# Head biases of an attention built once in an earlier layer and loaded by transfers

## The reference

```python
DILATED_GROUPS = ((128, 1), (512, 4), (2048, 16))
delta = u + BLOCK - kk
band = (delta >= 0) & (delta <= window // dilation)
bias = -slopes[:, None, None] * (delta * dilation).astype(jnp.float32)[None]
sc = jnp.where(valid[:, None, None], sc + bias, -jnp.inf)
...
x = x + _rms_norm(mix, g[1])
ff = _swiglu(_rms_norm(x, g[2]), ffn_in_w[layer], ffn_out_w[layer])
x = x + _rms_norm(ff, g[3])
```

## Time and profile before

| | us |
|---|---|
| median of the runs | 2267.86 (2267.3 to 2268.08) |
| the profiled execution | 2266.35 |
| its span | 2264.6 |
| PE busy | 98% of the span |
| DVE busy | 74% |
| ACT busy | 43% |
| POOL busy | 21% |
| mean granted clock of PE | 0.997 |

### The profile page before, as it was taken

The page is one execution under the profiler, slowest core; times in us unless marked ns, Lnnn a source line. Parts: engine busy times, 40 slices in busy tenths (PEclk is TensorE's granted clock), DMA queues, the critical chain, the costliest instruction groups (busy, mean ns, idle before and its releaser), DMA issues. The chain is left out here.

```text
span 2264.6 us, 31165 instructions
## 1 busy us (share of the span) xinstructions
PE 2218.9 (98%) x10682; PEld 1855.2 (82%) x10682; DVE 1686.4 (74%) x2529; ACT 962.9 (43%) x1758; POOL 485.5 (21%) x416
## 2 busy tenths in 40 slices
PE   9999998999999999999999999999899999999998
PEld 7888887888888888877888888888788888888886
DVE  6988759777777667797677666676877777776768
ACT  4322345232222343564666566565533333323453
POOL 5000026333333100251000001002633333310113
PEclk9999999999999999999999999999999999999999
DMA  5122341333333487635333333234133333338774
GB/s 159 38 56 56 114 142 57 109 108 97 109 96 111 158 265 242 205 121 164 85 85 85 68 73 84 57 108 144 53 111 112 98 107 103 103 110 280 247 228 172
DMA packets 246013, 278.37 MB, mean 123 GB/s; under 512 B 18528, under 2 KB 157792, under 8 KB 243808
## 3 DMA queue, kind: packets, MB, share of 16 engines
q1 hardware_dynamic: 242656, 264.84, 38.4%
q10 hardware_dynamic: 3200, 11.54, 1.5%
HBM read 202.40 MB, written 48.76 MB: 111 GB/s over the span
## 5 line engine op out<-in xcount | busy, mean ns | idle before, releaser
L1256 PE MATMUL banks<-xb_mid,up_split 128*128 128x512 f32 x2064 | 477.5, 391 | 1.5 <-DVE up_split L2388 1.5
L1256 PEld LDWEIGHTS banks<-xb_mid,up_split 128*128 128x128 f32 x2064 | 388.5, 188 | 82.3 <-DVE up_split L2388 1.7
L1345 PE MATMUL banks<-down_split 128*128 128x512 f32 x1848 | 422.9, 390 | 4.6 <-DVE down_split L2756 3.2
L1345 PEld LDWEIGHTS banks<-down_split 128*128 128x128 f32 x1848 | 345.5, 188 | 80.6 <-DVE down_split L2756 7.7
L1256 PE MATMUL banks<-xb_low,up_split 128*128 128x512 f32 x1584 | 367.5, 390 | 5.7 <-DVE xb_low L2316 2.0
L1256 PEld LDWEIGHTS banks<-xb_low,up_split 128*128 128x128 f32 x1584 | 297.0, 188 | 68.8 <-DVE up_split L2388 5.4
L2756 DVE TENSOR_TENSOR down_split<-down_raw,down_split 128x1024 fp32r<-128x1024 f32 x154 | 198.1, 1287 | 107.7 <-ACT down_split L1963 107.4
L1963 ACT CAST down_split<-down_raw 128x1024 fp32r<-128x1024 f32 x154 | 162.1, 1053 | 204.0 <-PE banks L1345 168.6
L3397 POOL TENSOR_TENSOR sums<-raw_up 128x512 f32<-128x512 f32 x88 | 117.0, 1332 | 481.5 <-DMA raw_up<-in_ffn_in_w 255.4
L1390 PE MATMUL banks<-x_hi,w_second 128*128 128x512 f32 x672 | 176.4, 394 | 0.0
L3069 DVE CUSTOM_DVE_ANT_0 scores<-banks,bias 128x896 f32<-128x896 f32 (+7 forms) x128 | 96.7, 756 | 73.3 <-PE banks L1427 64.1
(11 more groups left out here) (229 smaller groups left out, 3616.7 us busy)
## 6 DMA issues: line engine op xcount, KB each, us to landing
raw_up<-in_ffn_in_w SPq DMA_DIRECT2D x88, 512.0 KB, 5.0
down_raw<-in_ffn_out_w SPq DMA_DIRECT2D x154, 256.0 KB, 3.4
down_raw<-hid_spill SPq DMA_DIRECT2D x154, 256.0 KB, 4.1
hid_spill<-hid_mix SPq DMA_DIRECT2D x110, 256.0 KB, 4.7
down_second<-in_ffn_out_w SPq DMA_DIRECT2D x66, 256.0 KB, 3.4
k_stack<-k_parts SPq DMA_DIRECT2D x32, 512.0 KB, 6.3
hid_spill<-hid SPq DMA_DIRECT2D x44, 256.0 KB, 2.0
raw_up<-in_conv_in_w SPq DMA_DIRECT2D x18, 512.0 KB, 5.1
```

Source lines behind the costliest of these rows:

```text
L1256: mm = pe.matmul(bank(b_out), up_part(ph, p, a)[:, q * P:(q + 1) * P], block(RIGHT_OF[p], b)[:, q, :], start=(i == 0), stop=(i == len(pass ...
L1345: mm = pe.matmul(bank(b_out), side[:, a, 0, i * P:(i + 1) * P], side[:, b, 1, :], start=(p in (M3, M5, M1, M2) and first and j == 0), stop ...
```

## The change

The tables move from the opening of attention into up0. There the residual stream `resid` lies idle, so its eight tiles are stored to `x_keep`, and the tables take its place. POOL makes the iota in set 2; DVE works through 22 parts in sets 3 to 13, three in an odd set (two in set 13) and one in an even one: six parts for `dist`, the counts and the logarithms, then one part for each of the 16 heads, a full bias of 128x1024 in one instruction into one of two slots of `head_table`, which SP stores to `bias_spill`. In sets 15 to 18 SP loads the tiles of `resid` back. In attention `bias` has two slots, one for each head of a pair, filled by SP (`load_bias`): the first two behind the last transpose of norm2, the others behind the last maximum of the head that used the slot. DVE only waits for them; `head_bias`, `last_bias` and `slope` go. Before the last pair the second chunk of output weights is loaded ahead of the pair's first bias. The order `OPENING` is as before.

```diff
+        dist_i = at(112, "dist_i", [SEQ], I32)
+        neg_log = at(116, "neg_log", [SEQ])
+        counted = at(124, "counted", [2, SEQ])
+        head_table = at(136, "head_table", [2, SEQ])
+        TABLE_SETS, TABLE_PARTS, TILES_BACK = range(3, 14), 6, {15: (0, 1), 16: (2, 3), 17: (4, 5), 18: (6, 7)}
+        def table_parts(n):
+            before = 4 * ((n - 3) // 2) + (3 if n % 2 == 0 else 0)
+            return before, {2: 0, 3: 1, 4: 2} if n % 2 and n < 13 else {2: 0, 3: 1} if n % 2 else {3: 0}
...
+                if layer == 0:
+                    for t in range(TT):
+                        sp.wait_ge(*x_new_right.at("norm1", t + 1))
+                        sp.dma_start(x_keep[t], resid[:, t, :]).then_inc(kept, 16)
...
+                            if j >= TABLE_PARTS:
+                                head = j - TABLE_PARTS
+                                sp.wait_ge(*bias_made.at("up0", head + 1))
+                                sp.dma_start(bias_spill[head], head_table[:, head % 2, :]) \
+                                    .then_inc(bias_out[head % 2], 16)
+                    if layer == 0 and n in TILES_BACK:
...
+                        for t in TILES_BACK[n]:
+                            sp.dma_start(resid[:, t, :], x_keep[t]).then_inc(x_back, 16)
...
+            def load_bias(r, e):
+                moving, fixed = r
+                if fixed:
+                    sp.wait_ge(*max_done.at("attn", moving * STEPS + (fixed * STEPS - (1 - e) * TT)))
...
+                sp.dma_start(att["bias"][:, e, :], rows[bass.ds(moving * (2 * P) + (2 * fixed + e) * P, P), :]) \
+                    .then_inc(bias_in[e], 16)
...
-            for pos in range(2, 5):
+            for pos in range(2, 4):
                 load_projection(pos)
+            sp.wait_ge(*xt_turned.at("norm2", TT))
+            for e in range(2):
+                load_bias((0, 0), e)
+            load_projection(4)
             stack_first()
             for pair in range(PAIRS - 2):
                 load_projection(6 + 3 * pair)
                 load_projection(7 + 3 * pair)
                 stack_keys((0, pair + 1), 0)
+                load_bias((0, pair + 1), 0)
                 load_projection(8 + 3 * pair)
                 stack_queries((0, pair + 1), 0)
                 stack_keys((0, pair + 1), 1)
+                load_bias((0, pair + 1), 1)
                 stack_queries((0, pair + 1), 1)
             load_row_block("oproj", o_w[0], 0)
             stack_keys((0, PAIRS - 1), 0)
             load_row_block("oproj", o_w[0], 1)
+            load_bias((0, PAIRS - 1), 0)
             stack_queries((0, PAIRS - 1), 0)
             stack_keys((0, PAIRS - 1), 1)
+            load_bias((0, PAIRS - 1), 1)
...
+                    head = j - TABLE_PARTS
+                    if head >= 2:
+                        dve.wait_ge(bias_out[head % 2], 16 * (head // 2))
+                    dve.scalar_tensor_tensor(out=head_table[:, head % 2, :], in0=dist,
+                                             scalar=2.0 ** (-(head % 2 + 1) / 2 - head // 2), in1=logs,
+                                             op0=ALU.mult, op1=ALU.add).then_inc(bias_made.sem, 1)
...
-                    in1=att["bias"][:, SEQ - n:SEQ], scale=1.0, scalar=3e38,
+                    in1=att["bias"][:, place(s, last)[1], SEQ - n:SEQ], scale=1.0, scalar=3e38,
...
-                        head_bias(moving, fixed + (s + 1) // STEPS, (s + 1) // TT % 2, 0)
+                    if s + 1 in (TT, STEPS):
+                        dve.wait_ge(bias_in[(s + 1) // TT % 2],
+                                    moving * 16 + 16 * (fixed + (s + 1) // STEPS + 1))
...
-            distances()
-            window_counts(0)
-            window_counts(1)
             project((0, 0), 2, OPENING)
             prepare(chunk0["attn"] + 3)
             values_low((0, 0), 0, TURN)
-            window_counts(2)
             project((0, 0), 3, OPENING)
-            masked_logs()
-            log_of(2)
             prepare(chunk0["attn"] + 4)
             values_low((0, 0), 1, TURN)
-            log_of(3)
-            head_bias(0, 0, 0, 0)
-            head_bias(0, 0, 0, 1)
             project((0, 0), 5, OPENING)
+            dve.wait_ge(bias_in[0], 16)
             negated_scores(0, 0)
...
+                    if ph == "up0" and n == 2:
+                        pool.wait_ge(kept, 16 * TT)
...
+                        pool.iota(dist_i[:], pattern=[[-1, SEQ]], base=SEQ - P, channel_multiplier=1) \
+                            .then_inc(dist_ready.sem, 1)
```

More of the change, by code:

```diff
@@ L331, in trunk @@
         spilled, stored = sem("spilled"), sem("stored")
+        kept, x_back = sem("kept"), sem("x_back")
+        bias_out = [sem(f"bias_out{i}") for i in range(2)]
+        bias_in = [sem(f"bias_in{e}") for e in range(2)]
         k_stacked = [sem(f"k_stacked{e}") for e in range(2)]
@@ L843, in load_ffn @@
                         store_mixed(up, n - 1)
+                    if layer == 0 and n in TABLE_SETS:
+                        before, places = table_parts(n)
+                        for j in range(before, before + len(places)):
+                            if j >= TABLE_PARTS:
[4 more added lines that the diff above has]
+                    if layer == 0 and n in TILES_BACK:
+                        for b in range(2):
+                            sp.wait_ge(bias_out[b], 16 * PAIRS)
+                        sp.wait_ge(kept, 16 * TT)
+                        for t in TILES_BACK[n]:
+                            sp.dma_start(resid[:, t, :], x_keep[t]).then_inc(x_back, 16)
                     store_hidden(up, n)
@@ L2792, in mix, with table, window_counts @@
                 ins.then_inc(mix_made.sem, 1)
+            dist, logs, bits = dist_f[:], neg_log[:], window_bits[:]
+            rest, count = counted[:, 0, :], counted[:, 1, :]
+            tables = [0]
+            def table(ins):
+                ins.then_inc(table_step.sem, 1)
+                tables[0] += 1
+                dve.wait_ge(*table_step.at("up0", tables[0]))
+            def window_counts(n):
+                window, dilation = DILATED_GROUPS[n]
+                this = rest if n else count
+                if dilation == 1:
+                    table(dve.tensor_scalar(this, dist, float(window), None, ALU.is_le))
+                else:
+                    table(dve.tensor_scalar(bits, dist_i[:], dilation - 1, None, ALU.bitwise_and))
+                    table(dve.tensor_scalar(this, bits, 0.0, None, ALU.is_equal))
+                    if window < SEQ:
+                        table(dve.scalar_tensor_tensor(out=this, in0=dist, scalar=float(window),
+                                                       in1=this, op0=ALU.is_le, op1=ALU.mult))
+                if n:
+                    table(dve.tensor_tensor(count, count, rest, ALU.add))
@@ new lines, in distances, with masked_logs, log_of @@
+            def distances():
+                dve.wait_ge(*dist_ready.at("up0", 1))
+                table(dve.tensor_copy(dist, dist_i[:]))
+            def masked_logs():
+                table(dve.scalar_tensor_tensor(out=count, in0=dist, scalar=0.0, in1=count,
+                                               op0=ALU.is_ge, op1=ALU.mult))
+                table(dve.tensor_scalar(logs, count, 0.0, MASKED, ALU.is_equal, ALU.mult))
+            def log_of(c):
+                table(dve.tensor_scalar(rest, count, float(c), -float(np.log(c)),
+                                        ALU.is_equal, ALU.mult))
+                table(dve.tensor_tensor(logs, logs, rest, ALU.add))
@@ L2828, in up_layer @@
                         split_low(down, 1)
+                    if layer == 0 and n in TABLE_SETS:
+                        before, places = table_parts(n)
+                        if p in places:
+                            table_part(before + places[p])
                     if n and n % 2 and p == 1:
@@ L3115, in attend @@
                     project((0, fixed), 5)
-                    biases = 0
                     for s in range(STEPS):
-                        if s + 1 in (HT, TT, TT + HT):
-                            dve.wait_ge(*max_done.at("attn", steps + (s + 1)))
-                            for part in range(1 if s + 1 == HT else 2):
-                                biases += 1
-                                last_bias(place(s + 1, last)[1], part, biases)
+                        if s + 1 == HT:
+                            dve.wait_ge(bias_in[1], 16 * PAIRS)
                         if s + 1 < STEPS:
@@ L3451, in _ @@
             down_layer("down0", "norm2")
-            pool.wait_ge(*down_lo.at("down0", 2 * QN))
-            pool.iota(dist_i[:], pattern=[[-1, SEQ]], base=SEQ - P, channel_multiplier=1) \
-                .then_inc(dist_ready.sem, 1)
             def scale_pair(moving, fixed):
```

94 lines of the change are left out of this document (29 added, 65 removed).

## The result

| | before | after |
|---|---|---|
| median of the runs, us | 2267.47 (2266.29 to 2268.08, 8 runs) | 2274.09 (2273.42 to 2275.34, 8 runs) |
| the profiled execution | 2266.35 | 2273.42 |
| its span | 2264.6 | 2271.6 |
| PE busy | 2218.9 | 2222.3 |
| DVE busy | 1686.4 | 1676.8 |

The ratio after to before is 1.0030, with a 95% interval from 1.0021 to 1.0039: 6.6 us slower where 2.7 was forecast. That is inside the range, and beyond the 2272.4 us from which it counts as slower; the mechanism that was named as likeliest is not the one that carries it.

A forecast was written before the change was run, and what follows sets the result against it. PE was taken as the bound, busy 2218.9 of 2264.6 us. Opening +3.3, up projection +0.3 and last pair -0.9 summed to +2.7 us on the median 2267.86, so 2270.5 us; range 2265.5 to 2275.0.

The forecast's parts named there:

- the mechanism that was named as likeliest: Opening of attention: two bias loads lengthen the full transfer queue, so `q_stack` lands 2.3 us later; the forecast's chance 0.42.
- Part 4: First up projection: DVE's table work is nearly all hidden; +0.3 us booked, bounds 0 and +3.
- the cover: First up projection: DVE lateness that costs PE nothing, 4.0 us; 5.9 us of DVE waits hide work in an odd set.
- rival B: First up projection: DVE lateness passes 4.0 us, PE stalls 0.5 us in each of ten sets; 2275.3 us, chance 0.16.
- Part 1: Opening of attention: without table work on DVE the maximum comes earlier; 0.46 us gained at the transposes, bounds 0 to 0.75.
- Part 2: Opening: two 512 KB bias loads join the backlog begun by x_spill; `q_stack` 2.3 us later, bounds 0 and 2.6.
- the fall: Opening: PE's 3.2 us wait for `q_stack` makes the clock fall once more, booked at 1.5 us.
- A: Rival in the opening: the backlog is not prolonged, opening -0.5 us; total 2266.8 us, chance 0.17.
- C: Rival in the opening: POOL's scaling does not block DVE and the clock stays up; 2263.2 us, chance 0.07.
- Part 3: End of norm2: POOL's earlier scaling blocks DVE's last tile, 0.9 us later, not added because transfers set the wait's end.
- Part 5: Inside attention: biases by transfer gain nothing in the middle; -0.9 us booked in the last pair, bounds -1.5 and 0.
- both signs of being wrong: PE's `q_stack` wait under 1.2 us (then A or C); PE waiting over 2 us on line 1256, 430-640 us (then B).

The follow-up runs named there:

- e1_ring: The changed kernel with four slots for head tables in place of two: 2270.59 us, 1.0011 of the kernel before.
- e2_lock: The changed kernel, but POOL's first weight scaling in norm2 waits until DVE has scaled the last token tile: 2274.27 us, 1.0027 of the kernel before.
- e8_all: The changed kernel with the edits of e5_spread, e4_lock_late and e6_last all together: 2265.95 us, 0.9996 of the kernel before.
- e12_all_again: e8_all unchanged, run a second time against the kernel before: 2265.92 us, 0.9990.
- e3_late: The changed kernel, but only 256 KB of the first pair's biases load ahead of the stacks, 768 KB behind the query stacks: 2272.62 us, 1.0022.
- e4_lock_late: The changed kernel with the edits of both e2_lock and e3_late: 2271.86 us, 1.0019 of the kernel before.
- e6_last: The changed kernel, but the last pair's first bias loads behind its first query stacks, not ahead: 2274.46 us, 1.0031 of the kernel before.
- e5_spread: The changed kernel with its 22 table parts spread over sets 3 to 17, resid back in sets 18 to 20: 2269.33 us, 1.0012.

## Why the prediction came out as it did

**Part 4, the up projection: the step that failed.** +0.3 was booked and 5.15 measured, beyond its bound of +3. The collision in set 3 happened (`counted` took 2.20 us, and 1.23 when it ran again at 440.52), and the sums began at 442.39, 2.9 us later than in rows 9. In set 4 they began at 462.67, 4.1 us behind the product's end (439.51 + 19.04), where the text had 3.65 of 4.0, and PE lost 0.57 us; so by these rows the cover is nearer 3.5 us than 4.0, and e1_ring's 1.08 us is what this part costs without a slot wait. That three heads in a set are covered was right, as e1_ring shows. What failed was "the third waits until the first of them is stored, some 2 us". The length of a store was taken from how long DVE had waited for another (rows 9, 3.70), which says when a wait ends and not how long a store lives. In the queue the store stands behind 1 MB of weights, issued 2.6 us ahead of it, and lands in 6.7 us (5.3 in sets 9 and 11); DVE waits 4.73. With 4.73 in place of 2, set 7 comes to 8.4 us of delay for 5.9 of cover and PE has to stop; DVE waits 3.0 us for a slot in set 9 as well, and about as long in set 11. The text named stalls as rival B and gave them 5 us. B's sign was met (three waits of 3.3 us in all on this line) and its total fits, but not its account: it had 0.5 us in each of ten sets from a second collision, and most of the loss came in two jumps of 2.0 and 1.5 us behind the slot waits of sets 7 and 9.

**Part 1, the tables leave the opening.** The chain was right: the exponential starts at 1057.06, 0.02 us behind the end of its table load. But from the first use of `q_stack` to the transposes 3.15 us pass, against 3.31 before, so 0.16 us were gained and not 0.46; ACT's half of `q_parts` began 0.69 us behind PE's first use of `q_stack`, 0.47 before.

**Part 2, the biases in the transfer queue: mechanism right, its weight and its start wrong.** The text lets the backlog begin with `x_spill`. In the kernel before, `x_spill` had landed at 1030.5 (1017.63 + 12.9), 0.2 us behind the issue of the first key stack, so the end was set by the stacks themselves. With both biases ahead of the stacks `x_spill` takes 15.3 to 17.0 us in five profiles (16.6 after), and then it does reach into them. e1_ring, in which PE came early, is the case that the forecast had in mind: `q_stack` 2.8 us later behind `x_spill` than before (2.3 booked), PE waiting 2.68 us in one piece (3.2), and the clock down behind it:

```profile
1051.00:1053.00 2.00, 2.00 (x6) 1.71 (x7) 0.73 (x2) 1.34 (x2) 1.19 (x1) 0.50 0.00 1
```

The six matmuls behind it take 2.87 us and not 1.58. But from the first use of `q_stack` to the first transposed exponential it is 3.44 us, against 3.15 after and 2.94 to 3.43 in the ten other variants: the fall costs 0.5 us at most, and not the 1.5 booked, since PE has the maximum and the exponential to wait for anyway. And in the changed kernel itself the wait was 0.78 us, under the mark of 1.2 that the text had set, so by its own sign A or C would have held. Neither did. PE was late by itself, and what was booked in one place was paid in another.

**Part 3, the lock: size right, its place in the sum wrong.** +0.9 forecast, 0.92 measured, and by e2_lock's trace it is the lock. It was "not added", since the transfers would hide it. It hid the transfers as much as they hid it, and the larger of the two counts.

**The clock.** The forecast took one fall to be a price of 1.5 us. Over all profiles the stretch behind the same idle time comes in three lengths (below), and the changed kernel's had the long one, 1.46 us more than before. It can't be laid to the change: e1_ring, whose kernel is the same from there on, had 8.86 us. So the opening lost 2.1 us by stages (0.92 + 1.46 - 0.24) where 3.3 was booked, with other terms.

**Part 5.** The middle was put at nothing and gained 0.74 us, some 0.1 for each pair, and 0.69 to 0.87 in all twelve profiles; no run tests why. The last pair was put at -0.9 and lost 0.35: the wait near 1501 fell only from 0.73 to 0.37 us, and the bias loaded beside the output-weight chunk brought a new one of 0.96, which the text had put at zero, with a bound of +1, because "a load has half a pair to land". It asked whether the load is late, and not whom it makes late.

**The sum.** 5.15 + 2.14 - 0.74 + 0.35 + 0.1 = 7.0, against 0.3 + 3.3 - 0.9 = 2.7. The up projection is off by 4.9 us, more than the whole; the opening is off by -1.2, the middle by -0.7 and the last pair by +1.25. The measured 2274.09 us lies inside the range of 2265.5 to 2275.0 by luck: the range reached so far up for the near half of B, the step that decided was put at 0.3 us, and both signs of being wrong were met. In rival C the terms named sum to -3.9 us, 2264.0; the -4.7 beside it has no working.

## What to carry to other kernels

A ring of two slots that a transfer empties has to be costed with the time from issue to landing behind whatever stands in the queue at that moment (here 5.3 to 6.7 us behind 1 MB of weights, 2.6 with nothing ahead), and not with a wait seen elsewhere; where cover is short, spread the steps until no step reuses a slot in its own period. Work put on an idle engine or an idle queue is free only if nobody shares a port or a transfer with it: ask of every load whom it delays. Where two delays meet in one wait, removing one can show nothing; test them as a square.

## What the runs showed of the hardware

The stretch of 32 matmuls behind the idle time at the end of norm2 took 7.40 us in one profile (clock 1.00 throughout), 8.75 to 9.04 in seven and 9.79 to 10.28 in five, and the idle ahead of it does not sort them: 2.71 us stands ahead of 7.40 and of 8.75, 2.36 ahead of 8.82, 9.00 and 10.28. One stage varies by 2.9 us by the clock alone. In the opening the granted clock stayed at 1.00 behind the wait of 1.99 us in e2_lock and fell to 0.50 behind that of 2.68 in e1_ring. The Trainium skill, "TensorE: Matmul & The Clock Gate", section "What's actually happening", says that the count of slow matmuls differs from run to run of one kernel. It says so of the start of a kernel; here the same is seen in the middle of kernels that differ in other places, while the two profiles of one kernel, e8_all and e12_all_again, took 9.04 and 8.75 us.

The same up projection, with two slots, lost 5.15, 5.15, 7.17, 6.12 and 4.58 us in five profiles (after, e2_lock, e3_late, e4_lock_late, e6_last), though none of these edits touches it; with the parts spread out (e5_spread and the five built on it) the down projection started at 785.0 us, to 0.1, in all six. A kernel that waits for a transfer's landing inherits its spread.

While key and query stacks are under way the transfer share reads 1.0 at only 221 GB/s, half of the 408 that `x_spill` moves at the same share (rows 3). A share of 1 says that the queue is full, not how fast it empties.
